# Hidden activations of fourteen experts: turned by VectorE and carried between partitions by DMA, in place of TensorE transposes

## The reference

```python
def expert_choice_ffn(h, router_w, w_gate, w_up, w_down):
    cap = EC_CAPACITY * n // N_EXPERTS                 # 64 of 512 tokens
    aff = jax.nn.softmax(jnp.einsum('nd,de->ne', xf, router_w).astype(jnp.float32), axis=-1)
    gate, idx = lax.top_k(aff.T, cap)
    xs = xf[idx]
    hid = jax.nn.silu(jnp.einsum('ecd,edf->ecf', xs, w_gate)) * jnp.einsum('ecd,edf->ecf', xs, w_up)
    out = jnp.einsum('ecf,efd->ecd', hid, w_down) * gate[..., None].astype(xs.dtype)
    y = jnp.zeros_like(xf).at[idx.reshape(-1)].add(out.reshape(-1, D).astype(xf.dtype))
```

## Time and profile before

| | us |
|---|---|
| median of 3 runs | 1548.56 |
| lowest, highest | 1548.12, 1549.33 |
| the profiled execution, its own time | 1548.32 |
| its span in the trace | 1546.5 |
| TensorE busy in the span | 1535.3 (99%) |
| VectorE busy | 1310.5 (85%) |
| ScalarE busy | 1043.1 (67%) |
| GpSimd busy | 223.1 (14%) |
| moved by DMA | 498.60 MB, mean 322 GB/s |

### The profile page before, as it was taken

How to read it: one execution, slowest core, us unless ns; L and a number is a source line. 1 busy time by engine, 2 the same in 40 slices (tenths; PEclk the granted TensorE clock), 3 DMA queues, 4 the chain that set the end, 5 groups by cost and what they waited for, 6 DMA issues and landing times.

```text
span 1546.5 us, 22686 instructions
## 1 busy us (share of the span) xinstructions
PE 1535.3 (99%) x8378; PEld 1241.3 (80%) x8378; DVE 1310.5 (85%) x1386; ACT 1043.1 (67%) x985; POOL 223.1 (14%) x140
## 2 busy tenths in 40 slices
PE   9999999999999999999999999999999999999998
PEld 7888888888873888888888888888888888888886
DVE  7684786685766899999999999999999999999987
ACT  6453556343453777777777777777777777777777
POOL 0000001000022222120212202022120302210003
PEclk9999999999999999999999999999999999999999
DMA  9543438333466999999999999999999999999998
GB/s 343 188 139 115 154 137 280 102 123 99 146 238 233 397 420 403 402 401 382 413 380 393 393 386 415 376 406 386 395 402 369 417 382 405 388 386 408 363 393 340
DMA packets 156407, 498.60 MB, mean 322 GB/s; under 512 B 10880, under 2 KB 36608, under 8 KB 156352
## 3 DMA queue, kind: packets, MB, share of 16 engines
q1 hardware_dynamic: 144624, 461.54, 77.0%
q0 software_dynamic: 9280, 31.07, 6.5%
q10 hardware_dynamic: 2448, 5.25, 1.3%
HBM read 473.70 MB, written 20.97 MB: 320 GB/s over the span
## 4 chain that ended last, share of the span: by engine, by line
PE 96%; DMA 1%; ACT 1%; DVE 1%; SPq 0%; issue 0%; POOLq 0%; POOL 0%; DVEq 0%; ACTq 0%
PE ps L1974 82%; PE ps L2022 4%; PE ps L2113 2%; PE ps L2029 2%; PE ps L2071 2%; PE ps L2082 1%; PE ps L2430 1%; PE ps L2279 1%; DMA u_rows<-arena 1%; DMA raw<-w_qkv 1%; PE ps L2567 0%; PE ps L2275 0%; PE ps L2297 0%; DMA xh<-u_rows,first_rows_at 0%; SPq L588 0%
## 5 line engine op out<-in xcount | busy, mean ns | idle before, releaser
L1311 DVE TENSOR_TENSOR w_rest<-raw,w_high 128x2048 fp32r<-128x2048 f32 x212 | 506.9, 2402 | 65.8 <-ACT w_high L1188 48.3
L1188 ACT CAST w_high<-raw 128x2048 fp32r<-128x2048 f32 x184 | 352.5, 1916 | 139.5 <-PE ps L1974 139.4
L1974 PE MATMUL ps<-w_high,xt_high 128*128 128x512 f32 x984 | 304.8, 390 | 0.0
L1974 PE MATMUL ps<-w_rest,xt_high 128*128 128x512 f32 x984 | 304.6, 389 | 0.0
L1974 PE MATMUL ps<-w_high,xt_rest 128*128 128x512 f32 x984 | 304.5, 389 | 0.0
L1974 PEld LDWEIGHTS ps<-w_high,xt_high 128*128 128x128 f32 x984 | 184.7, 188 | 39.0 <-issue 0.8
L1311 DVE TENSOR_TENSOR w_rest<-early,w_high 128x2048 fp32r<-128x2048 f32 x90 | 206.7, 2299 | 10.7 <-ACT w_high L1188 10.7
L1974 PEld LDWEIGHTS ps<-w_high,xt_rest 128*128 128x128 f32 x984 | 184.8, 188 | 38.3
L1974 PEld LDWEIGHTS ps<-w_rest,xt_high 128*128 128x128 f32 x984 | 184.8, 188 | 38.3
L1311 DVE TENSOR_TENSOR w_rest<-raw_more,w_high 128x2048 fp32r<-128x2048 f32 x92 | 206.6, 2283 | 6.1 <-ACT w_high L1188 6.1
L1188 ACT CAST w_high<-early 128x2048 fp32r<-128x2048 f32 x90 | 172.3, 1915 | 58.1 <-PE ps L1974 58.1
(11 more groups left out here) (310 smaller groups left out, 2211.8 us busy)
## 6 DMA issues: line engine op xcount, KB each, us to landing
raw<-w_down SPq DMA_DIRECT2D x64, 1024.0 KB, 8.3
raw<-w_gate SPq DMA_DIRECT2D x62, 1024.0 KB, 8.4
raw<-w_up SPq DMA_DIRECT2D x62, 1024.0 KB, 8.1
raw_more<-w_down SPq DMA_DIRECT2D x32, 1024.0 KB, 8.4
early<-w_down SPq DMA_DIRECT2D x32, 1024.0 KB, 8.9
raw_more<-w_gate SPq DMA_DIRECT2D x31, 1024.0 KB, 9.0
raw_more<-w_up SPq DMA_DIRECT2D x31, 1024.0 KB, 8.8
early<-w_gate SPq DMA_DIRECT2D x31, 1024.0 KB, 9.0
```

Source lines behind the costliest of these rows:

```text
L1188: nc.scalar.copy(w_high[:, i % SLOTS, :], src).then_inc(high_done, 1)
L1311: nc.vector.tensor_tensor(w_rest[:, j, :], src, w_high[:, j, :].bitcast(F32), ALU.subtract).then_inc(rest_done, 1)
L1974: done = nc.tensor.matmul(out, lhs, rhs, start=start and part == 0, stop=stop and part == 2)
```

## The change

The hidden activations of experts 1 to 14 are no longer turned by TensorE. The steps that take the place of `all_turns`:

- VectorE turns each half (128x1024) in 32x32 blocks within its partitions: `turn_hidden`, into `blocks` (`arena[:, 0:2]`).
- SP asks for 16 transfers for each half (`move`), each of 32 partitions x 256 columns (32 KB, in rows of 1 KB), from `blocks` to `shuffled` (`arena[:, 2:4]`), from quarter a of the partitions to quarter c, for all a and c. Each adds to the semaphore `hid_moved`.
- ScalarE makes the high part from there (`moved_high`) and VectorE the rest (`moved_rest`), reading SBUF in place of PSUM, each at a place of its own in the order.
- The rows of w_down of experts 1 to 14 are put in the matching order before the launch (`down_by_blocks`); the loads keep their size and shape.

The banks of gate and up change for the second half (gate in banks 6 and 7, up in 0 and 1), which the transposes no longer use, and TensorE's waits with them. The rows of tokens are multiplied by the norm's weights after they are turned, by ScalarE, in eight activations of 128 columns (`weigh_rows`, into `h_more[:, 0]`), and GpSimd's multiplication goes; VectorE's `turn_rows` waits for the gather itself. The four small loads of the weights' pieces become one.

```diff
+            def move(e, h, lo, hi):
+
+                if lo == 0:
+                    sp.wait_ge(turned_step, hid_turned(e, h))
+                for n in range(lo, hi):
+                    a, c = n // QUARTERS, n % QUARTERS
+                    tokens = blocks[a * QUARTER:(a + 1) * QUARTER, h, c * SPAN:(c + 1) * SPAN]
+                    place = shuffled[c * QUARTER:(c + 1) * QUARTER, h, a * SPAN:(a + 1) * SPAN]
+                    sp.dma_start(place, tokens).then_inc(hid_moved, 16)
+
+            def load_and_move(f):
+
+                load_run(f, 8, gate_up_rows, f + 1, 0, GU_PAIRS)
+                load_run(f, 16, down_rows, f, 0, 1)
+                move(f, 1, 0, 8)
...
             with sp.Fori(1, E - 2) as f:
-                load_run(f, 8, gate_up_rows, f + 1, 0, GU_PAIRS)
-                load_run(f, 16, down_rows, f, 0, 1)
-                load_run(f, 17, gate_up_rows, f + 1, 1, GU_PAIRS)
+                load_and_move(f)
+                load_run(f, 17, gate_up_rows, f + 1, 1, 1)
+                move(f, 1, 8, MOVES)
+                load_run(f, 17, gate_up_rows, f + 1, 1, GU_PAIRS, 1)
                 load_run(f, 24, down_rows, f, 0, D_PAIRS, 1)
-                load_run(f, 28, down_rows, f, 1, D_PAIRS)
+                load_run(f, 28, down_rows, f, 1, 2)
+                move(f + 1, 0, 0, 5)
+                load_run(f, 28, down_rows, f, 1, 3, 2)
+                move(f + 1, 0, 5, 10)
+                load_run(f, 28, down_rows, f, 1, D_PAIRS, 3)
+                move(f + 1, 0, 10, MOVES)
...
-                pool.wait_ge(gathered, 16 + 16 * QUARTERS * (e + 1))
-                tokens = xg.rearrange("p (t n) -> p t n", t=QUARTERS)
-                weights = piece_g.rearrange("p (t n) -> p t n", t=1).broadcast_to([P, QUARTERS, SPAN])
-                nc.gpsimd.tensor_tensor(tokens, tokens, weights, ALU.mult).then_inc(rows_scaled, 1)
...
+            def weigh_rows(e):
+                act.wait_ge(turned_step, rows_turned(e))
+                act.wait_ge(xtr_done, e + 1)
+                for k in range(KC):
+                    at = slice(k * P, (k + 1) * P)
+                    nc.scalar.activation(weighted_rows[:, at], turned_rows[:, at], ACT.Copy, scale=piece_g[:, k:k + 1]).then_inc(rows_scaled, 1)
...
+            def moved_high(e, h):
+                act.wait_ge(hid_moved, 16 * MOVES * (2 * e + h - 1))
+                nc.scalar.copy(chunks(ht[h][0]), from_shuffled(h)).then_inc(hth_done, 1)
...
+            def turn_hidden(e, h):
+                if not (isinstance(e, int) and e == 1 and h == 0):
+                    dve.wait_ge(hid_moved, 16 * MOVES * (2 * e + h - 2))
+                dve.wait_ge(hid_done, 2 * e + h + 1)
+                nc.vector.transpose(blocks[:, h, :], acts[h]).then_inc(turned_step, 1)
+
+            def moved_rest(e, h):
+                dve.wait_ge(hth_done, 2 * e + h + 1)
+                nc.vector.tensor_tensor(chunks(ht[h][1]), from_shuffled(h), chunks(ht[h][0]).bitcast(F32), ALU.subtract).then_inc(htr_done, 1)
...
             with pe.Fori(1, E - 2) as f:
-                gate_up(f, 8, (xtr_done, f + 3), (htr_done, 2 * f + 1))
+                pe.wait_ge(hid_done, 2 * f + 2)
+                gate_up(f, 8, (0, 2), (xtr_done, f + 3))
                 pe.wait_ge(ys_done, f + 1)
                 down(2 * f, 0, f, 16, 0, 1)
-                gate_up(f, 17, (silu_done, 2 * f + 3), (hid_done, 2 * f + 3))
+                gate_up(f, 17, (6, 0), (silu_done, 2 * f + 2), (silu_done, 2 * f + 3))
                 down(2 * f, 0, f, 24, 1, 4)
-                all_turns(f + 1)
                 down(2 * f + 1, 1, f, 28)
```

More of the change, by code:

```diff
@@ L290, in encoder_kernel @@
         spread_rows = lg
-        piece_g = grow[:, 0:SPAN]
+        piece_g = mx[:, :, :].rearrange("p a i -> p (a i)")
+        weighted_rows = h_more[:, 0, :]
         quadrant = var[:, 27:28]
@@ L299, in encoder_kernel @@
         acts = (silu, hid)
+        blocks = arena[:, 0:2, :]
+        shuffled = arena[:, 2:4, :]
         ht = ((ht_high, ht_rest), (odd_high, odd_rest))
@@ L450, in body_turn, with rows_turned, hid_turned @@
             return GU_PAIRS // RAW_SLOTS + (2 * (GU_PAIRS + D_PAIRS) // RAW_SLOTS) * e + i // RAW_SLOTS
+        def rows_turned(e):
+            return 1 if isinstance(e, int) and e == 1 else 3 * e - 3
+        def hid_turned(e, h):
+            return 3 * e - 1 + 2 * h
         def pairs_before(e):
@@ L1148, in step_silu @@
                     return
-                nc.scalar.activation(acts[odd], bank(0, 2), ACT.Silu).then_inc(silu_done, 1)
+                nc.scalar.activation(acts[odd], bank(gate_bank, 2), ACT.Silu).then_inc(silu_done, 1)
             def rows_high(e):
@@ L1155, in rows_high @@
                     return
[L1156 to L1157 removed]
+                act.wait_ge(rows_scaled, KC * e)
+                nc.scalar.copy(xt_high[:, :], weighted_rows).then_inc(xth_done, 1)
+            def weigh_rows(e):
+                if isinstance(e, int) and e == 1:
+                    act.wait_ge(grow_in, 16 * 2)
+                act.wait_ge(turned_step, rows_turned(e))
[3 more added lines that the diff above has]
+                    nc.scalar.activation(weighted_rows[:, at], turned_rows[:, at], ACT.Copy, scale=piece_g[:, k:k + 1]).then_inc(rows_scaled, 1)
             def hidden_high(s, odd, banks=6, used_by_down=None):
@@ L2392, in _ @@
                 _, last = early_gate_up(kc)
-            last.then_inc(early_done, 1)
+            last.then_inc(early_mm, 1)
             def early_third(lo, hi):
```

162 lines of the change are left out of this document (92 added, 70 removed).

## The result

| | before | after |
|---|---|---|
| median, us | 1548.76 | 1608.87 |
| lowest, highest | 1548.12, 1549.33 | 1604.79, 1612.33 |
| runs | 4 | 4 |

The ratio is 1.0387, with a 95% interval of 1.0362 to 1.0412. The profiled execution of after took 1609.47 us, its span is 1607.6. Slower was forecast, but the time lies above the range (1538 to 1602).

The account below looks back on a forecast made before the run. TensorE was taken to set the 66.67 us round, and DMA to set 69.0 (64.0 + 5.0) after the change. 30.3 for 13 rounds - 2.9 - 1.4 = +26.0 on 1548.56 gave 1574.6 us, range 1538 to 1602.

Parts of the forecast that it names:

- The bound and where it moves: Whole loop: TensorE sets the 66.67 us round, DMA has 2.7 us of room; with the transfers DMA sets 69.0 us.
- The signs named for it: Rounds of about 69 us, landings near 18 us, TensorE waiting for `w_rest`, VectorE for ScalarE, ScalarE for `raw<-` transfers.
- Parts 1 to 3: Transposes leave TensorE: 19.3 us, round 65.29; VectorE needs 63.4 us a round, ScalarE 54 to 57, both hidden.
- Part 4: On SP: 32 more issues a round at 0.37 us, 12 us, covered by SP's 52 us of waits; no landing moves.
- Part 5: At the DMA engines: 32 transfers, 1.05 MB a round, cost 5.0 us at 208 GB/s; little chance above 7 us.
- Rival 5: Moves cost 7 us or more, or their late arrival stalls ScalarE: +51 at 7 us, 1600 and above; chance 0.10.
- Rival 1: Moves run near the full rate, 2.5 to 3.3 us a round: 1543 to 1553 us; chance 0.20.
- defer 2.9 us: DMA queue grows from 15.9 us to the 18.8 that eight buffers allow before TensorE waits: 2.9 us off the sum.
- the block ahead of it: The fourteenth block, ahead of the loop, loses its transposes too and gives 1.4 us.
- 2: DMA has room after all, so TensorE stays the bound and all of 14 x 1.38 is kept: 1529 us; chance 0.09.
- 3: A clump on VectorE and ScalarE overruns the 4.0 us slack by some tenths a round: 1534 us; chance 0.04.
- 4: Moves cost between 3.3 and 4.3 us, partly overlapped halves: 1553 to 1565 us; chance 0.12.

## Why the prediction was wrong, point by point

**The bound and where it moves.** Right. TensorE set the round before, DMA had some 3 us of room a round (66.67 - 63.5 = 3.2, and not 2.7), and with the transfers DMA sets it. The signs named for it are there: landings that don't fall (medians of 13.7 to 18.8 us, near the named 18 for `early` only), TensorE waiting for `w_rest`, ScalarE for loads.

**Parts 1 to 3.** Right. TensorE's round without the transposes is 65.28 for 65.29 predicted, and 1528.59 for the 1529 of a kernel that they alone would make. The stalled subtraction is gone and the eight activations take 0.3 us each (0.36 estimated). VectorE, then ScalarE:

```profile
1052.16 8.88 DVE L1372 TENSOR_TENSOR w_rest<-raw,w_high 128x2048 fp32r<-128x2048 f32 x4
...
1051.63 2.44 ACT L1206 ACTIVATE h_more<-v,mx 128x128 f32<-128x128 f32 x8
```

**Part 4, SP.** The issue was taken at 0.37 us from rows of single loads. The five groups of transfers take SP 26 us a round and not 12. One issue took at least 507 ns, in the median 592 and at most 2718:

```profile
L660 SPq DMA_DIRECT2D arena<-arena x448: 507/592/2718, 551.8 to 1509.4; - x150
```

The short series outside the loop have the same median (594 ns), so the form costs more than a load's 373; the long ones are found where the queue is long, and there a load's issue grows too (`raw<-w_up` up to 2.8 us, in before 0.46). The issues stayed mostly hidden, as said, but not for nothing: they are 9% of the chain, and on GpSimd's queue the round is 0.9 us shorter.

**Part 5, the transfers.** This is the step that failed, as a term mis-sized. The sum has 64.0 + 5.0 = 69.0 us for a round; it was 70.63, the mean of 13, and 71.3 at the start. In the kernel's terms: 63.5 + 7.1. The 5.0 came from a copy alone in flight, and in a full queue with idle engines 1.05 MB in this form indeed cost 5.2 to 5.9. In the loop they cost 7.1 to 7.5, some 0.5 to 0.8 of it with the engines at work, and the rest of the difference has no shown cause. The reasoning "with several loads queued the engines have other work meanwhile", on which little chance was given to 7 us and more, was wrong: the rate falls to 229 to 333 GB/s in most slices with narrow transfers in flight, though the share stays full. Rival 5 had the cost (7 us for 7.1). That its total of +51 is what the 13 rounds lost, 51.6, is chance: its rounds alone were to lose 56.3, and its total stands against a measured +61. Rival 1, at the full rate, holds for wide transfers only.

**The sum's other terms.** The queue was to grow before TensorE waits and to defer 2.9 us. The first round was already 71.27, so nothing was deferred. And the sum ended with the loop, while the part after it took 10.2 us more. Of these, 2.3 lie before the next activation (45.75 us for 43.49), where the last half's sixteen transfers stand, and 8.0 behind it. The chain of after shows there what was waited for:

```profile
1549.44 13.93 DMA h_rows<-xh,rows
...
1572.97 18.04 DMA early<-w_down
...
1591.15 8.84 PE ps L2641 x24
```

SP asks for the last pair of w_down behind its wait for the adding of expert 14's result, which took 13.9 us to land in the long queue, and behind issues that this queue held up. So that pair is asked for 24.9 us after the activation, in before 16.8 (1494.91 to 1511.69), which is the 8 us.

The forecast of +26.0 against +61.1 for the spans is thus short by 35.1 us: 21.3 in the rounds (the 5.0 us), 2.9 for the deferral that didn't come, 10.2 behind the loop, and 0.7 of the 1.4 for the block ahead of it.

**Rivals.** 2 had the right price of a kernel with room, 1529, and a wrong premise. 3 doesn't occur (rounds of 65.28 without transfers). 4 is ruled out by 7.1 us. The range left most of rival 5 out at a chance of 0.10, and its upper end took the middle of the unknown cost for its bound: the far bound of 11.8 us was worked out and then not used.

## What to carry to other kernels

When DMA has little room, price every added transfer inside the loop that it joins: put the transfers into the kernel before with nobody waiting for them, and the round tells their cost (1607.7 us here for the 1608.9 of the finished change). Keep copies within SBUF as wide as the partitions go and their rows at 1 KB or more; narrow transfers, which carrying data between quarters of the partitions needs, cost nearly three times a copy of all partitions with the same bytes in this loop, and twice outside of it. After a change of bound, count the part behind the loop too, since the loop hands its full queue to it: here the last load stood behind an issue and a wait that the queue made 8 us longer.

## What the runs showed of the hardware

- 1.05 MB within SBUF beside the loads of the loop: 2.4 to 2.9 us over 128 partitions with rows of 1 or 4 KB, 7.1 to 8.6 over 32 or 64 partitions, 11.5 over 128 partitions with rows of 256 bytes (some of it gaps in the queue). Beside loads alone: 2.6 to 2.8 and 5.1 to 5.9. Engine time with nothing beside it: 3.0 over 128 partitions, 4.6 over 32 or 64, 4.7 over 128 with rows of 256 bytes.
- A DMA share of 1.03 stood at 421, 412, 385 and 379 GB/s alike (loads only; one wide transfer a half; the change; narrow transfers in place): it doesn't tell a well filled queue from a badly filled one.
- With TensorE, VectorE and ScalarE busy in SBUF, narrow transfers with rows of 1 KB went from 404 to 398 GB/s of the mix, and loads (421, 421) and wide ones (419, 419) stayed.
- SP's issue of a transfer of 32 x 256 within SBUF took 0.59 us in the median and up to 2.7 in the loop. A load's took 0.37 in the median, and up to 2.8 (`raw<-w_up`) behind a long queue.
